# Turning the differential probabilities with VectorE and DRAM instead of TensorE, and their value products placed later

## The reference, cut to what matters

```python
h = rms_norm(x, pre_w, NORM_EPS)
proj = jnp.einsum('bsd,dn->bsn', h, w_in)
...
p = jax.nn.softmax(sc, axis=-1)              # differential mixer: two maps per head
attn = p[:, :, 0] - lam * p[:, :, 1]
return jnp.einsum('bhqk,bkhe->bqhe', attn, vf)
...
_, idx = lax.top_k(score, n_sel)             # sparse mixer: 64 keys per query
...
mix = jnp.concatenate([oa, ob], axis=-1)
y = jnp.einsum('bsm,md->bsd', mix, w_out)
return x + rms_norm(y, post_w, NORM_EPS)
```

## Time and profile before

| | |
|---|---|
| median of 3 runs | 303.1 us (302.99 to 303.43) |
| profiled execution | 302.85 us, span 301.1 us |
| PE busy | 292.4 us, 97% |
| PEld busy | 246.4 us, 82% |
| DVE busy | 234.9 us, 78% |
| ACT busy | 163.9 us, 54% |
| POOL busy | 67.6 us, 22% |
| DMA | 60.01 MB, mean 199 GB/s |

### The profile page before, as it was taken

The page is one execution under the profiler, slowest core; times in us unless marked ns, Lnnn a source line. Parts: engine busy times, 40 slices in busy tenths (PEclk is TensorE's granted clock), DMA queues, the critical chain, the costliest instruction groups (busy, mean ns, idle before and its releaser), DMA issues.

```text
span 301.1 us, 4401 instructions
## 1 busy us (share of the span) xinstructions
PE 292.4 (97%) x1568; PEld 246.4 (82%) x1568; DVE 234.9 (78%) x474; ACT 163.9 (54%) x284; POOL 67.6 (22%) x116
## 2 busy tenths in 40 slices
PE   8999999999999999999999999999999999999992
PEld 7799777788787888788888988778878788887892
DVE  4752989899999997955984786878999999787343
ACT  5986963736577473603665855473737747390101
POOL 6558210303030220101060740012303030210101
PEclk9999999999999999999999999999999999999998
DMA  7999959457518569860059799937653675742011
GB/s 242 370 371 386 371 214 354 135 143 227 195 69 210 209 211 303 191 201 23 0 158 369 242 350 250 325 108 204 209 150 131 146 272 152 202 70 72 0 70 70
DMA packets 62229, 60.01 MB, mean 199 GB/s; under 512 B 34560, under 2 KB 39424, under 8 KB 62208
## 3 DMA queue, kind: packets, MB, share of 16 engines
q1 hardware_dynamic: 61920, 59.47, 62.8%
q10 hardware_dynamic: 288, 0.26, 0.3%
HBM read 54.48 MB, written 5.24 MB: 198 GB/s over the span
## 4 chain that ended last, share of the span: by engine, by line
PE 40%; DVE 37%; ACT 8%; DMA 6%; POOL 4%; issue 3%; SPq 1%; POOLq 0%; DVEq 0%; ACTq 0%
DVE w_lo L987 14%; PE bank_a L470 8%; PE bank_a L461 7%; PE bank_a L466 7%; PE bank_s L618 6%; DMA w_raw<-in_w_in 6%; PE bank_a L618 5%; ACT xt_pbuf L831 4%; DVE work L1107 4%; DVE xt_pbuf L1124 3%; DVE top L1106 3%; DVE xt_pbuf L1140 3%; DVE mixn L1150 2%; DVE mixn L1036 2%; PE bank_s L559 1%
## 5 line engine op out<-in xcount | busy, mean ns | idle before, releaser
L987 DVE TENSOR_TENSOR w_lo<-w_raw,w_hi 128x2048 fp32r<-128x2048 f32 (+1 forms) x46 | 98.8, 2154 | 18.5 <-ACT w_hi L763 18.3
L763 ACT ACTIVATE w_hi<-w_raw 128x2048 fp32r<-128x2048 f32 (+1 forms) x46 | 81.9, 1784 | 31.9 <-PE bank_a L470 23.4
L461 PE MATMUL bank_a<-w_hi,h_hi 128*128 128x512 f32 (+1 forms) x272 | 72.5, 388 | 0.0
L470 PE MATMUL bank_a<-w_lo,h_hi 128*128 128x512 f32 (+1 forms) x272 | 70.0, 379 | 0.5 <-DVE w_lo L987 0.5
L466 PE MATMUL bank_a<-w_hi,h_lo 128*128 128x512 f32 (+1 forms) x272 | 69.9, 379 | 0.0
L470 PEld LDWEIGHTS bank_a<-w_lo,h_hi 128*128 128x128 f32 x272 | 49.7, 188 | 10.5 <-DVE w_lo L987 1.0
L466 PEld LDWEIGHTS bank_a<-w_hi,h_lo 128*128 128x128 f32 x272 | 49.8, 188 | 9.8
L461 PEld LDWEIGHTS bank_a<-w_hi,h_hi 128*128 128x128 f32 x272 | 47.9, 188 | 10.4 <-issue 2.7
L831 ACT ACTIVATE xt_pbuf<-xt_pbuf,st 128x128 f32<-128x128 f32 (+1 forms) x48 | 21.3, 444 | 25.1 <-DVE st L1124 25.1
L1417 POOL TENSOR_TENSOR rt<-nat,tab 128x256 f32<-128x256 f32 x10 | 7.4, 741 | 112.5 <-ACT nat L815 112.5
L815 ACT ACTIVATE nat<-bank_a,st 128x512 f32<-128x512 f32 x20 | 13.5, 681 | 19.6 <-PE bank_a L470 19.6
(11 more groups left out here) (196 smaller groups left out, 431.1 us busy)
## 6 DMA issues: line engine op xcount, KB each, us to landing
w_raw<-in_w_in SPq DMA_DIRECT2D x30, 1024.0 KB, 6.0
w_raw<-in_w_out SPq DMA_DIRECT2D x8, 1024.0 KB, 6.1
w_raw<-in_w_in SPq DMA_DIRECT2D x8, 584.0 KB, 7.3
turned<-mixn SPq DMA_DIRECT2D x20, 128.0 KB, 2.7
prm<-in_rows SPq DMA_DIRECT2D x2, 705.0 KB, 7.0
w_raw<-in_w_in SPq DMA_DIRECT2D x2, 512.0 KB, 6.3
xres<-in_x SPq DMA_DIRECT2D x2, 512.0 KB, 9.5
dqT<-turned SPq DMA_DIRECT2D x2, 512.0 KB, 5.9
```

Source lines behind the costliest of these rows:

```text
L461: pe.matmul(bank, h_hi[:, HALF * half + kk, tok], whi[:, kk, :], start=half == 0 and kk == 0, stop=False)
L470: mm = pe.matmul(bank, h_hi[:, HALF * half + kk, tok], wlo[:, kk, :], start=False, stop=half == 1 and kk == HALF - 1)
L763: act.activation(unit(w_hi, u), unit(raw, u), ACT.Copy).then_inc(hi_done.sem, 1)
L987: dve.tensor_tensor(unit(w_lo, u), unit(raw, u), unit(w_hi, u).bitcast(F32), ALU.subtract).then_inc(lo_done.sem, 1)
```

## The change

The three turns of differential probabilities leave PE. DVE now turns the 32x32 squares of PD0, PD1A and PD1B, each straight after its `combine` (PD0 after the squares of the sparse queries, two steps later); SP writes each to DRAM with four DMAs and reads it back into `pT` with one. The three copies from bank T go. To have room, the squares of the sparse queries are written to `iqT`, where the turned sparse keys come later, so `drain_pair(T_SK)` now also waits until these squares are in DRAM.

On PE, `values(0)` moves from behind `dsa_scores(12)` to behind `first(18)`, and `values(1)` from behind `dsa_scores(14)` to behind `turn_mix(T_MD0)`. On DVE, one `choose` round moves from before `combine(10)` to after it, and `gate_dsa(0)` moves ahead of `drain_mix(T_MD1)`. `gathered` only names a slot of a flat tile; the slots are contiguous as they were, and the DRAM pieces keep their 128 bytes.

```diff
-T_IK, T_DK, T_PD0, T_PD1A, T_SK, T_PD1B = 4, 5, 7, 8, 9, 11
-T_MD0, T_MD1, T_MS0, T_MS1 = 12, 13, 14, 15
-T_USES = 16
-PS0, PS1 = range(3, 5)
+T_IK, T_DK, T_SK = 4, 5, 7
+T_MD0, T_MD1, T_MS0, T_MS1 = 9, 10, 11, 12
+T_USES = 13
+IQS, DQS, SQS, PD0, PD1A, PD1B, PS0, PS1 = range(8)
+SLOT = {PD0: 0, PD1A: 1, PD1B: 2, PS0: 0}
 LANES = 32
 SQUARES = P // LANES
...
         rd, rs = st[:, 154:156], st[:, 156:158]
         squares = mixn[:, :, :].rearrange("p b n -> p (b n)")
-        prob_buf = {PS0: dkT[:, 0:2, :].rearrange("p f t -> p (f t)"), PS1: dqT[:, :, :, :].rearrange("p b f t -> p (b f t)")}
+        prob_buf = {PD0: mixn[:, 0, :], PD1A: nat[:, 1, 0, :], PD1B: nat[:, 1, 1, :], PS0: dkT[:, 0:2, :].rearrange("p f t -> p (f t)"), PS1: dqT[:, :]}
 
 
...
         pool_setup = sem("pool_setup")
 
-        ends = (S[1], T[0])
+        ends = (S[1], T[1])
         last_ms = st[:, 153:154]
 
...
                 put(n, prob_buf[n], prob_put[n].sem)
 
             def get_probs(layer, n):
                 sp.wait_ge(prob_put[n].sem, prob_put[n].at(layer, 16 * SQUARES))
 
-                sp.wait_ge(o_filled.sem, o_filled.at(layer, 1 if n == PS0 else 2))
-                dst = pT[:, 0, :] if n == PS0 else pT[:, 1:3, :].rearrange("p s n -> p (s n)")
-                sp.dma_start(dst, scratch[n].rearrange("p a t -> p (a t)")).then_inc(prob_landed[n].sem, 16)
+                if n >= PS0:
+                    sp.wait_ge(o_filled.sem, o_filled.at(layer, 1 if n == PS0 else 2))
+                dst = pT[:, 1:3, :].rearrange("p s n -> p (s n)") if n == PS1 else pT[:, SLOT[n], :]
+                sp.dma_start(dst, scratch[n].rearrange("p s t -> p (s t)")).then_inc(prob_landed[n].sem, 16)
 
...
-                        put(1, squares, dq_put.sem)
+                        put(DQS, squares, dq_put.sem)
                     if u == 14:
                         sp.wait_ge(dq_put.sem, dq_put.at(layer, 16 * SQUARES))
-                        get(1, dqT, dq_landed.sem)
+                        get(DQS, dqT, dq_landed.sem)
                     if u == 16:
                         sp.wait_ge(sq_squares.sem, sq_squares.at(layer, 1))
-                        put(2, squares, sq_put.sem)
+                        put(SQS, iqT, sq_put.sem)
+                        put_probs(layer, PD0)
                     if u == 17:
                         sp.wait_ge(sq_put.sem, sq_put.at(layer, 16 * SQUARES))
-                        get(2, sqT, sq_landed.sem)
+                        get(SQS, sqT, sq_landed.sem)
+                        put_probs(layer, PD1A)
+                        get_probs(layer, PD0)
+                    if u == 18:
+                        put_probs(layer, PD1B)
+                        get_probs(layer, PD1A)
+                        get_probs(layer, PD1B)
...
                 first(14)
                 second(14)
                 first(15)
-
-                pe.wait_ge(combined.sem, combined.at(layer, 1))
-                turn_probs(T_PD0, 6, 0, HEADS)
                 diff_scores(10, 1, (2, 3))
                 second(15)
-
-                pe.wait_ge(combined.sem, combined.at(layer, 2))
-                turn_probs(T_PD1A, 8, 1, 2)
                 first(16)
                 second(16)
                 turn_nat(T_SK, 0, 5)
                 first(17)
 
-                pe.wait_ge(combined.sem, combined.at(layer, 3))
-                turn_probs(T_PD1B, 10, 1, 2)
-
                 pe.wait_ge(t_drained.sem, t_drained.at(layer, T_SK + 2))
                 pe.wait_ge(sq_landed.sem, sq_landed.at(layer, sq_landed.per_layer))
                 dsa_scores(12, 0, range(HEADS))
-                pe.wait_ge(t_drained.sem, t_drained.at(layer, T_PD0 + 1))
-                values(0, 0, v_diff, [[slot(0, h)] for h in range(HEADS)], place(layer, DV, 0) + 1)
                 second(17)
                 first(18)
+
+                pe.wait_ge(prob_landed[PD0].sem, prob_landed[PD0].at(layer, 16))
+                values(0, 0, v_diff, [[gathered(pT[:, 0, :], h, slots=HEADS)] for h in range(HEADS)], place(layer, DV, 0) + 1)
                 dsa_scores(13, 1, (0, 1))
                 dsa_scores(14, 1, (2, 3))
-                pe.wait_ge(t_drained.sem, t_drained.at(layer, T_PD1B + 1))
-                values(1, 1, v_diff, [[slot(1 + h // 2, 2 * (h % 2) + t) for t in range(2)] for h in range(HEADS)],
-                       place(layer, DV, 1) + 1)
                 second(18)
                 turn_mix(T_MD0, 0, 0)
+
+                pe.wait_ge(prob_landed[PD1A].sem, prob_landed[PD1A].at(layer, 16))
+                pe.wait_ge(prob_landed[PD1B].sem, prob_landed[PD1B].at(layer, 16))
+                values(1, 1, v_diff, [[gathered(pT[:, 1 + h // 2, :], 2 * (h % 2) + t, slots=HEADS) for t in range(2)] for h in range(HEADS)],
+                       place(layer, DV, 1) + 1)
                 first(19)
                 second(19)
                 turn_mix(T_MD1, 1, 1)
 
                 pe.wait_ge(prob_landed[PS0].sem, prob_landed[PS0].at(layer, 16))
-                values(2, 0, v_dsa, [[slot(0, h)] for h in range(HEADS)], place(layer, SV, 0) + 1)
+                values(2, 0, v_dsa, [[gathered(pT[:, 0, :], h, slots=HEADS)] for h in range(HEADS)], place(layer, SV, 0) + 1)
 
                 pe.wait_ge(t_drained.sem, t_drained.at(layer, T_MD0 + 1))
                 out_part(0, 0, 0)
...
-                    dve.transpose(squares, nat[:, slot, :, :].rearrange("p b n -> p (b n)")).then_inc(done, 1)
+                    dve.transpose(iqT[:, :] if rope == 4 else squares, nat[:, slot, :, :].rearrange("p b n -> p (b n)")).then_inc(done, 1)
 
                 def turn_probs(n, use):
-                    dve.wait_ge(exps_done.sem, exps_done.at(layer, use + 1 - S_DIFF0))
-                    probs = pbuf[:, 0, :] if n == PS0 else pbuf[:, 1:3, :].rearrange("p s n -> p (s n)")
+                    if n >= PS0:
+                        dve.wait_ge(exps_done.sem, exps_done.at(layer, use + 1 - S_DIFF0))
+                    else:
+                        dve.wait_ge(combined.sem, combined.at(layer, n - PD0 + 1))
+                    probs = pbuf[:, 1:3, :].rearrange("p s n -> p (s n)") if n == PS1 else pbuf[:, use % 4, :]
                     dve.transpose(prob_buf[n], probs).then_inc(prob_squares.sem, 1)
...
-                    if j in (10, 11):
-
-                        dve.wait_ge(t_filled.sem, t_filled.at(layer, T_PD0 + 1))
+                    if j in (10, 12, 14):
+
+                        dve.wait_ge(prob_squares.sem, prob_squares.at(layer, {10: 1, 12: 2, 14: 3}[j]))
...
 
                 mask_scores(8, 1, 2, causal[:, :])
                 mask_scores(9, 1, 2, causal[:, :])
+                turn_squares(1, 4, sq_squares.sem)
                 dve.wait_ge(dq_put.sem, dq_put.at(layer, 16 * SQUARES))
-                turn_squares(1, 4, sq_squares.sem)
+                turn_probs(PD0, 6)
                 split_lo(layer, 16)
                 combine(8, 1, 2, 0)
-
-                drain(T_PD0, pT[:, 0, :])
+                dve.wait_ge(sq_squares.sem, sq_squares.at(layer, 1))
+                turn_probs(PD1A, 8)
+
                 mask_scores(10, 1, 2, causal[:, :])
                 mask_scores(11, 1, 2, causal[:, :])
                 split_lo(layer, 17)
+                choose(1, 1)
+                combine(10, 1, 2, 2)
+                turn_probs(PD1B, 10)
                 choose(1, 2)
-                drain(T_PD1A, pT[:, 1, :])
-                combine(10, 1, 2, 2)
-                choose(1, 1)
                 mask_unchosen(1)
+
+                dve.wait_ge(sq_put.sem, sq_put.at(layer, 16 * SQUARES))
                 drain_pair(T_SK, skT)
                 split_lo(layer, 18)
-
-                drain(T_PD1B, pT[:, 2, :])
                 mask_scores(12, 0, 4, work[0][:, :])
                 split_lo(layer, 19)
                 turn_probs(PS0, 12)
                 gate_diff(1)
                 split_lo(layer, 22)
 
+                gate_dsa(0)
                 drain_mix(T_MD1, m_hi, m_lo, 1, subln)
-                gate_dsa(0)
                 drain_mix(T_MS0, h_hi, h_lo, 0)
                 split_lo(layer, 23)
                 gate_dsa(1)
```

More of the change, by code:

```diff
@@ L240, in build_trunk @@
         rq_ready = count("rq_ready", BLOCKS)
-        prob_squares = count("prob_squares", 2)
-        prob_put = {n: count(f"prob_put{n}", 16 * SQUARES) for n in range(PS0, PS1 + 1)}
-        prob_landed = {n: count(f"prob_landed{n}", 16) for n in range(PS0, PS1 + 1)}
+        prob_squares = count("prob_squares", 5)
+        prob_put = {n: count(f"prob_put{n}", 16 * SQUARES) for n in range(PD0, PS1 + 1)}
+        prob_landed = {n: count(f"prob_landed{n}", 16) for n in range(PD0, PS1 + 1)}
         subln_ready = count("subln_ready", 1)
@@ L317, in put @@
                 for i in range(SQUARES):
[L318 to L319 removed]
+                    to = scratch[n].rearrange("(j r) s (i c) -> i r s j c", j=SQUARES, i=SQUARES)[i]
```

(18 more changed lines are left out.)

24 lines of the change are left out of this document (12 added, 12 removed).

## The result

The changed kernel takes 305.63 us (305.45 to 305.72) against 303.05 us: ratio 1.0082, 95% interval 1.0064 to 1.0099. It is slower, as forecast, but by 2.6 us where 0.9 was forecast, and the time lies above the range.

What follows compares the result with a forecast made beforehand. PE was taken as packed, with DVE close beside it; MS0 starting 0.45 us later per layer gave +0.9 us, so 302.85 became 303.75 profiled, and a median 0.25 above it, 304.0 us. Range 301.0 to 305.4.

Steps and rivals of the forecast that it cites:

- Three PE transposes gone, 1.3 us, all lost again at the sparse keys: PE saves 0.44 us per transpose group, 1.3 per layer, but waits at the sparse keys; `dsa_scores(12)` starts 0.56 later.
- DVE's work ahead of the keys' copies, +0.87 us: Three square transposes replace two copies, 0.67 us, plus waits on itself; the sparse keys' copies end at 104.64.
- The two waits of DVE for its own result: DVE turns PD1A and PD1B straight after their `combine`, losing 0.1 us each, from 0 to 0.2.
- 0.2 more for POOL beside DVE's `combine`: Part of the upper bound, with own waits of 0.2: about +0.9 us per layer, 304.9 us.
- The copies' delay reaches PE and all behind it: `dsa_scores(12)` starts at 104.69, 0.56 us later; through gates and MD1, MS0 starts 0.45 later per layer.
- `values(0)` later: It ends at 111.97 against 105.84; POOL's first step takes 0.20, `gate_diff(0)` comes 1.24 us later, MD1 waits 0.6.
- `gate_dsa(0)` earlier, the old wait goes: DVE's gate ends at 128.15, so PE's old wait of 0.5 to 0.7 us ahead of MS0 goes.
- DMAs hidden: 12 more writes and 3 more reads per layer on SP's queue hold nothing; sparse queries have least slack, 1.8 us.
- the waits did not cancel: Rival: PE's new waits and the saved work cancel exactly, 303.1 us; chance 0.20.
- PE kept nothing: Rival: PE keeps its gain with no wait at the keys or MD1, 299.1 us, or half, 301.1; chance 0.17.
- POOL's step was not 1.71 of its own: Rival: POOL's first step after `values(0)` really takes 1.71 us, `gate_diff(0)` 1.51 later still, 307.0 us; chance 0.05.
- no read-back held PE in the changed kernel: Rival: turned sparse queries land 2.8 us later than assumed, `dsa_scores(12)` slips 1.0 per layer, 306 us; chance 0.08.

Runs made afterwards that it cites:

- a_round2: The changed kernel with two `choose` rounds ahead of `combine(10)` and one behind: 304.70 us against 302.76 for the kernel before, ratio 1.0065.
- b_round1: The kernel before with only one `choose` round moved from ahead of PD1A's copy and `combine(10)` to behind them: 303.94 us against 302.76, ratio 1.0045.
- a_round3: The changed kernel with all three `choose` rounds ahead of `combine(10)`: 303.75 us, ratio 1.0032 to the kernel before.
- c_val0: The changed kernel with `values(0)` back behind `dsa_scores(12)`, ahead of `second(17)`: 304.59 us against 302.89 for the kernel before, ratio 1.0058.
- c_gate_old: The changed kernel with `gate_dsa(0)` back behind `drain_mix(T_MD1)`: 306.84 us against 302.89 for the kernel before, ratio 1.0129.
- c_nowrite: The changed kernel without the 12 new DRAM writes per layer and SP's waits for them to land: 305.62 us against 302.89 for the kernel before, ratio 1.0094.
- b_gate: The kernel before with only `gate_dsa(0)` moved ahead of `drain_mix(T_MD1)`: 301.23 us against 302.76, ratio 0.9955; again 301.48 against 302.93, 0.9947.

## Why the prediction was wrong

The sign and the chain of waits were right. One effect, POOL beside `combine(10)`, stood at nothing in the sum, and it was 0.88 us per layer. Point by point:

- *Three PE transposes gone, 1.3 us, all lost again at the sparse keys*: right. `turn_nat(T_SK)` waited for POOL as worked out (0.65 late, forecast 0.67).
- *DVE's work ahead of the keys' copies, +0.87 us*: this is the step that failed. It was +1.79. "Moving a `choose` round past `combine(10)` moves nothing at this point, since both stand ahead of it" counted the work and not what runs beside it: `combine(10)` came to begin inside POOL's rotary step and took 0.88 us more. (The two waits of DVE for its own result came out at 0.17 and 0.11 us, where 0.1 each was taken: 94.11 against 94.01 - 0.07, and 101.60 against 101.56 - 0.07.) The text allowed "0.2 more for POOL beside DVE's `combine`". The Trainium skill, page "SBUF — State Buffer", section "SBUF: two separate sides", has the rule in both directions, for a VectorE instruction with two SBUF inputs against a GpSimd one that reads SBUF: whichever starts first holds the ports. I weighed it only where DVE held up POOL. The traces agree with it: in a_round2 and b_round1 DVE instructions of 0.15 and 0.22 us last until POOL's ends, within 0.02 us.
- *The copies' delay reaches PE and all behind it*: right; a_round3, which takes the overlap away, measures the +0.3% that was forecast, and not by luck: its copies, 0.90 late, and its MS0, 0.52 late, stand where the chain had put them.
- *`values(0)` later*: right in kind (POOL's step short, DVE idle 2.13 us, forecast 2.2). That PE would wait at MD1 was right too (0.35 us, forecast 0.6). The move costs 0.4 to 0.5 us per layer (c_val0).
- *`gate_dsa(0)` earlier, the old wait goes*: right, alone 1.5 us over both layers, in the changed kernel 1.4 (c_gate_old).
- *DMAs hidden*: right for the change (c_nowrite). The slack that was named, 1.8 us at the sparse queries, is not the one that a faster order used up. Those were the read-backs of PS0 and PS1, which the prediction did not work out; SP reads PS0 4.7 us later than before (122.00 - 117.05 - 0.22).

The rivals: the waits did not cancel, PE kept nothing, POOL's step was not 1.71 of its own, and no read-back held PE in the changed kernel. The bounds were too narrow above, since the price of POOL beside DVE was bounded by a guess instead of by the whole length of POOL's instructions, up to 0.74 us each, which the rows had shown.

## What to carry to other kernels

When two steps on DVE are swapped, their sum stays, but what POOL does meanwhile changes: lay POOL's timeline beside DVE's for each moved instruction that reads two SBUF operands, and price the overlap by up to the rest of POOL's instruction. Look for the one wait that is left on a packed engine first: exchanging two steps ahead of it (b_gate) gave 0.5% where the rebuilt transposes gave a loss. The work that was moved onto the DMA queue was free here only at the changed kernel's pace; measure it without the writes in the order one aims at, not only in the one that one has.

## What the runs showed of the hardware that was not expected

A DVE `scalar_tensor_tensor` on two columns, 0.15 us alone, took 0.63 us until POOL's elementwise instruction had ended. The other direction appears too: POOL's rotary multiply took 1.33 us instead of 0.74 when it came under `split_lo` 17. DVE's MAX8 and MATCH_REPLACE8, whose rows show one input of 128x256, were not stretched beside POOL (0.41 to 0.43 us beside it, 0.38 to 0.43 without). Such an overlap cost 0.5 to 0.9 us per layer, where the transposes that the change took from PE were 1.3.
